# Splitting the double step of a block inverse in two, with a new order table for the merged stage

## The reference

```python
def wkv_scan(r, decay, k, v, a, b, s0):
    def step(s, inp):
        r_t, w_t, k_t, v_t, a_t, b_t = inp
        sa = jnp.einsum('bhvk,bhk->bhv', s, a_t)
        s = s * w_t[:, :, None, :] + sa[..., None] * b_t[:, :, None, :] + v_t[..., None] * k_t[:, :, None, :]
        return s, jnp.einsum('bhvk,bhk->bhv', s, r_t)
```

```python
past = cache_kv[l, page_table].reshape(DB, -1, 4, NSA_KV_HEADS, HEAD_DIM)
```

## Time and profile before

| | |
|---|---|
| median of 3 runs | 2172.32 us (2167.52 to 2173.0) |
| the profiled execution | 2170.53 us |
| its span, first to last instruction | 2168.6 us |
| TensorE matmul busy | 1960.5 us (90%) |
| VectorE busy | 1231.5 us (57%) |
| ScalarE busy | 702.4 us (32%) |
| mean granted TensorE clock | 0.946 |

### The profile page before, as it was taken

One profiled execution on the slowest core, in us unless ns is written; L12 is line 12 of the kernel. 1 busy time (PEld: TensorE's weight loads), 2 busy tenths in 40 slices (PEclk: granted clock), 3 DMA queues, 4 the chain that ended last, 5 costly groups with the idle time before them and its releaser, 6 DMA issues.

```text
span 2168.6 us, 53451 instructions
## 1 busy us (share of the span) xinstructions
PE 1960.5 (90%) x22324; PEld 1804.1 (83%) x22324; DVE 1231.5 (57%) x2034; ACT 702.4 (32%) x1294; POOL 49.2 (2%) x137
## 2 busy tenths in 40 slices
PE   5999999988896999999769998999887979999995
PEld 5999888766696999999769987887666879999995
DVE  3254888887736444452333448888886364444423
ACT  3222333433334232342233223433334332222421
POOL 0000000000000101100000000000000000110000
PEclk9999899998998999999879998999998979999998
DMA  4224733232321323223132256332333212323232
GB/s 181 89 84 144 180 109 105 61 99 83 106 94 45 93 89 97 88 88 98 53 133 89 78 176 160 99 99 71 101 88 110 82 49 89 98 88 96 81 101 79
DMA packets 155835, 214.36 MB, mean 99 GB/s; under 512 B 21569, under 2 KB 121410, under 8 KB 153922
## 3 DMA queue, kind: packets, MB, share of 16 engines
q1 hardware_dynamic: 151682, 208.64, 31.5%
q10 hardware_dynamic: 3904, 2.23, 0.5%
HBM read 202.57 MB, written 16.59 MB: 101 GB/s over the span
## 4 chain that ended last, share of the span: by engine, by line
PE 64%; DVE 18%; SPq 8%; issue 4%; ACT 3%; DMA 3%; DVEq 0%; ACTq 0%; another core or an unknown queue 0%
PE ps L814 17%; PE ps L816 16%; PE ps L815 16%; SPq L704 7%; PE ps L1166 2%; DMA ring<-in_w 1%; DVE arena L1999 1%; PE ps L833 1%; DVE arena L1767 1%; DVE arena L1990 1%; PE ps L834 1%; DVE x L2179 1%; DVE arena L1904 1%; PE ps L1132 1%; PE ps L1047 1%
## 5 line engine op out<-in xcount | busy, mean ns | idle before, releaser
L1678 DVE TENSOR_TENSOR ring_lo<-ring,ring_hi 128x1024 fp32r<-128x1024 f32 x202 | 247.4, 1225 | 679.9 <-ACT ring_hi L1321 679.4
L814 PE MATMUL ps<-hm_hi,ring_hi 128*128 128x260 f32 x1600 | 456.1, 285 | 10.0 <-DVE hm_lo L1685 5.2
L816 PE MATMUL ps<-hm_hi,ring_lo 128*128 128x260 f32 x1600 | 454.7, 284 | 0.0
L815 PE MATMUL ps<-hm_lo,ring_hi 128*128 128x260 f32 x1600 | 453.3, 283 | 0.0
L1321 ACT ACTIVATE ring_hi<-ring 128x1024 fp32r<-128x1024 f32 x202 | 213.8, 1059 | 680.2 <-PE ps L816 615.7
L814 PEld LDWEIGHTS ps<-hm_hi,ring_hi 128*128 128x128 f32 x1600 | 304.1, 190 | 12.5 <-issue 7.3
L816 PEld LDWEIGHTS ps<-hm_hi,ring_lo 128*128 128x128 f32 x1600 | 303.7, 190 | 0.0
L815 PEld LDWEIGHTS ps<-hm_lo,ring_hi 128*128 128x128 f32 x1600 | 303.7, 190 | 0.0
L814 PE MATMUL ps<-in_hi,ring_hi 128*128 128x260 f32 x736 | 211.6, 287 | 6.9 <-DVE ring_lo L1678 6.9
L814 PE MATMUL ps<-hf_hi,ring_hi 128*128 128x260 f32 x704 | 202.1, 287 | 8.8 <-DVE hf_lo L1685 8.2
L816 PE MATMUL ps<-in_hi,ring_lo 128*128 128x260 f32 x736 | 207.8, 282 | 0.0
(11 more groups left out here) (401 smaller groups left out, 3354.5 us busy)
## 6 DMA issues: line engine op xcount, KB each, us to landing
ring<-in_w SPq DMA_DIRECT2D x202, 512.0 KB, 3.5
extra<-in_kv_cmp SPq DMA_DIRECT2D x96, 128.0 KB, 2.3
arena<-in_kv_cmp SPq DMA_DIRECT2D x80, 128.0 KB, 2.4
slot<-in_kv_cmp SPq DMA_DIRECT2D x80, 128.0 KB, 2.9
out_win_old<-in_win SPq DMA_DIRECT2D x16, 511.0 KB, 4.4
arena<-in_k_sel SPq DMA_DIRECT2D x96, 64.0 KB, 1.9
extra<-in_k_sel SPq DMA_DIRECT2D x96, 64.0 KB, 1.9
slot<-in_v_sel SPq DMA_DIRECT2D x96, 64.0 KB, 1.9
```

The source lines that it names most:

```text
L814: mmul(out, wh, hi[:, k, cols], start=(k == 0), stop=False)
L815: mmul(out, wh, lo[:, k, cols], start=False, stop=False)
L816: last = mmul(out, wl, hi[:, k, cols], start=False, stop=(ci == len(chunks) - 1 and k == k1 - 1))
L1678: v.tensor_tensor(ring_lo[:, n % RING, :], r, ring_hi[:, n % RING_HI, :], SUB).then_inc(S["w_lo"], 1)
```

## The change

The step `dbl` is split in `dblw` (bank 1, for the transposed inverse `ww`) and `dblz` (bank 0, for the inverse `zz`), and `add` in `addw` and `addz`. Level 5 has only the z half. The next level's `inv` waits for `addw` alone; `dblw` and `dblz` of a level wait for `addz` of the level before. The semaphores are now `inv_dw` and `inv_z` for w, `inv_d` and `inv_zz` for z. The same matmuls and adds are done. The order table is new as a whole.

```diff
         for lv in range(1, LEVELS):
-            put(("inv", lv), "PE", 1.08, *here(("add", lv - 1) if lv > 1 else "w0", ("maskb", 1)))
+            put(("inv", lv), "PE", 1.08, *here(("addw", lv - 1) if lv > 1 else "w0", ("maskb", 1)))
+            if lv > 1:
+                put(("addz", lv - 1), "DVE", 0.8, *here(("dblz", lv - 1)))
             put(("qmask", lv), "DVE", 0.84, *here(("inv", lv)))
-            put(("dbl", lv), "PE", 2.06 if lv < LEVELS - 1 else 1.05, *here(("qmask", lv), "zz", ("maskk", 1)))
-            put(("add", lv), "DVE", 1.43 if lv < LEVELS - 1 else 0.85, *here(("dbl", lv)))
+            if lv < LEVELS - 1:
+                put(("dblw", lv), "PE", 1.05, *here(("qmask", lv), ("maskk", 1), ("addz", lv - 1) if lv > 1 else "zz"))
+                put(("addw", lv), "DVE", 0.8, *here(("dblw", lv)))
+            put(("dblz", lv), "PE", 1.05, *here(("qmask", lv), ("addz", lv - 1) if lv > 1 else "zz", ("maskk", 1)))
+        put(("addz", LEVELS - 1), "DVE", 0.85, *here(("dblz", LEVELS - 1)))
...
-                    elif stage[0] == "dbl":
+                    elif stage[0] in ("dblw", "dblz"):
                         lv = stage[1]
                         if lv == 1:
                             pe.wait_ge(*at_sc("zz_ok", 1))
                             pe.wait_ge(*at_sc("gmask", 4))
+                        else:
+                            pe.wait_ge(*at_sc("inv_zz", lv - 1))
                         pe.wait_ge(*at_sc("inv_qc", lv))
                         for cj in range(2 * RJ):
                             c, j = divmod(cj, RJ)
                             for r in HP:
-                                last = mmul(ps[r, 0, cj * CH:(cj + 1) * CH], qq[r, c, j, :], zz[r, c, j, :], start=True, stop=True)
-                                if lv < LEVELS - 1:
+                                if stage[0] == "dblz":
+                                    last = mmul(ps[r, 0, cj * CH:(cj + 1) * CH], qq[r, c, j, :], zz[r, c, j, :], start=True, stop=True)
+                                else:
                                     last = mmul(ps[r, 1, cj * CH:(cj + 1) * CH], zz[r, c, j, :], qq[r, c, j, :], start=True, stop=True)
-                        last.then_inc(T["inv_d"], 1)
+                        last.then_inc(T["inv_d" if stage[0] == "dblz" else "inv_dw"], 1)
...
-                        pe.wait_ge(*at_sc("inv_z", LEVELS))
+                        pe.wait_ge(*at_sc("inv_zz", LEVELS - 1))
...
-                    elif stage[0] == "add":
-                        lv = stage[1]
-                        dve.wait_ge(*at_sc("inv_d", lv))
+                    elif stage[0] == "addw":
+                        dve.wait_ge(*at_sc("inv_dw", stage[1]))
+                        o.go(v.tensor_tensor(w8, w8, bank8(1), ADD))
+                        o.tell(T["inv_z"])
+                    elif stage[0] == "addz":
+                        dve.wait_ge(*at_sc("inv_d", stage[1]))
                         o.go(v.tensor_tensor(z8, z8, bank8(0), ADD))
-                        if lv < LEVELS - 1:
-                            o.go(v.tensor_tensor(w8, w8, bank8(1), ADD))
-                        o.tell(T["inv_z"])
+                        o.tell(T["inv_zz"])
```

In the table, the first line of digits is this:

```diff
-ORDER = ("008670667870768677066086067707700667767767777666070707668676070667786607700000777701716817177181767106167171718776717171"
+ORDER = ("807600786067708707760707706670777677078066707766708676776660876700670070707061617167161777107117687171161677187676176678"
```

More of the change, by code:

```diff
@@ L143 @@
           "gmm": 4, "gmask": 4, "nmm": 1, "inv_q": LEVELS - 1, "inv_qc": LEVELS - 1,
-          "inv_d": LEVELS - 1, "inv_z": LEVELS, "zz_ok": 1, "tm_mm": 3, "tm_ev": 3, "rh_mm": 2, "rh_ev": 2, "u_mm": 2,
+          "inv_d": LEVELS - 1, "inv_dw": LEVELS - 2, "inv_zz": LEVELS - 1, "inv_z": LEVELS - 1, "zz_ok": 1, "tm_mm": 3, "tm_ev": 3, "rh_mm": 2, "rh_ev": 2, "u_mm": 2,
           "u_ev": 2, "ds_mm": 2, "s_ok": 2, "y_ev": 1, "mean_mm": 1, "yc": 1, "var_mm": 1, "var_v": 2, "var_a": 1, "done": 1}
@@ L203, in rwkv_threads @@
         for lv in range(1, LEVELS):
-            put(("inv", lv), "PE", 1.08, *here(("add", lv - 1) if lv > 1 else "w0", ("maskb", 1)))
+            put(("inv", lv), "PE", 1.08, *here(("addw", lv - 1) if lv > 1 else "w0", ("maskb", 1)))
+            if lv > 1:
+                put(("addz", lv - 1), "DVE", 0.8, *here(("dblz", lv - 1)))
             put(("qmask", lv), "DVE", 0.84, *here(("inv", lv)))
-            put(("dbl", lv), "PE", 2.06 if lv < LEVELS - 1 else 1.05, *here(("qmask", lv), "zz", ("maskk", 1)))
-            put(("add", lv), "DVE", 1.43 if lv < LEVELS - 1 else 0.85, *here(("dbl", lv)))
+            if lv < LEVELS - 1:
[3 more added lines that the diff above has]
+        put(("addz", LEVELS - 1), "DVE", 0.85, *here(("dblz", LEVELS - 1)))
         for c in range(2):
-            put(("rhs", c), "PE", 1.6, *here(("state", 0) if c else ("add", LEVELS - 1), ("tmcopy", 2)))
+            put(("rhs", c), "PE", 1.6, *here(("state", 0) if c else ("addz", LEVELS - 1), ("tmcopy", 2)))
             put(("rhcopy", c), "ACT", 0.5, *here(("rhs", c)))
@@ L353, in early_thread @@
     return [(("early", 0, "whi"), "ACT", 1.15, [("smp", 6, "sel_v")]), (("early", 0, "wlo"), "DVE", 1.4, [("early", 0, "whi")])]
-ORDER = ("008670667870768677066086067707700667767767777666070707668676070667786607700000777701716817177181767106167171718776717171"
-         "761677877676766232732327732663677227326226872222617766372732726776262363772766672772362762672871161621717672716616671267"
-         "268812672767271167161276212272662866622672827216272772726474624227672272627762642223876677227767827743666237272732473362"
-         "766274633772267632762763273176267266772612772667772711167168261626271221728177617162812627227162786222762622342677262272"
-         "276646222886767264624662488426276766223632362266646663276822363621633687262636682231622171662166221126617711762676171767"
-         "211226212226667627272462762728262726722627428626727627272642726238624266628482736372638372762362263272642422622663322222"
-         "632236226264466744676654646877754767")
+ORDER = ("807600786067708707760707706670777677078066707766708676776660876700670070707061617167161777107117687171161677187676176678"
+         "777717726672336267267676362732762763222632226672622282238626723263212276233611667222212726112227227162661712276821176712"
+         "226776221721762217227222264473686728767662422767242776776272647776676762726277627267632633764276722368477662323812326867"
+         "233672731172276616771672726762276721272672278627122766727162126118617762272721276712212722267727666777672666774263646772"
+         "824467782267627482726267423622278223622622386362426363622262672683222132666822362367626212222621111186626121262221276671"
+         "121162272762612682242676228782222622776667246242772276786247726272762762677227782662622622663227624722623263632738223626"
+         "36282622732662262462647626623276362672683446648467676464655767467677")
 def merged_order():
```

## The result

The changed kernel is slower: 2181.53 us (median of 8 runs, 2179.24 to 2187.32) against 2171.04 us before, ratio 1.0051 with a 95% interval of 1.0041 to 1.0061. One execution in all that follows was slow (3114.87 us, of `split_old_pool`); medians and ratios leave it out. The forecast was 2171 us with a range of 2158 to 2184: the time lies in the range, but the direction is that of rival (b), which had put it at 2183. The profiled execution's span grew from 2168.6 to 2180.6 us.

A forecast was written before the change was run, and what follows sets the result against it. It took VectorE's steps, then SP's page loads, to bound each mixed stage. With `win_v` 0 8 us late, the layers gained 1.3 and 0.1 us: −1.4 on 2170.53, 2170.9 on the median's scale, so 2171 us, range 2158 to 2184.

The forecast's parts named there:

- rival (b): SP's ten units start too late for their pauses to cover, plus a new wait at the fifth `sel_k`: 2183 us, chance 0.24.
- I take `win_v` 0 as 8 us late: First window value product on TensorE, delayed by steps newly ahead on VectorE; 8 us, bounds 5 and 13.
- the end of each stage is the start of that fourth value unit plus 62 us: End of each mixed stage: five value units on SP's queue, of fixed length, follow that unit's start.
- the later of two things: Fourth value unit starts once SP is done with the ten units before it and `sel_v` 0 has been read.
- The steps counted ahead of the last VectorE step: VectorE before `win_v` 0: four moved steps, 8.5 and 1.0 us, and eight split adds, 1.9 us, make 11.4 us more.
- The cover of 2.3 us: Between `win_pt`'s end at 418.06 and `win_v` 0 at 420.32, behind other matmuls; taken off the 11.4 us, leaving 9.1.
- The idle time at the inverse that I gave back: TensorE's waits for VectorE at the `inv` and double lines, 9.3 us a layer, should fall to about 6.
- slack: SP's pause before the fourth value unit, 10.4 and 8.1 us beyond the 1.2, covers a later start of its ten units.
- 0.24 us for each of 16 levels: VectorE's two split add steps of 0.84 us replace one of 1.44, adding 3.8 us a layer.
- Some 3 us lower: If the split cost VectorE nothing, the shift would be 1.9 us smaller and the result some 3 us lower.
- Rival (a): The inverse's chain holds the first half; `win_v` 0 is late by only 3 to 4 us: 2161 us, chance 0.28.
- Rival (c): The split acts on nothing and the table's shifts cancel: 2172 us, chance 0.48 together with the forecast.

The follow-up runs named there:

- `split_old_pool`: Split code in the old order, with every second page transfer of the selected units issued from GpSimd's queue in place of SP's; 2155.91 us, ratio 0.9935.
- `before_late24`: The kernel before with only the sample's steps put later in the merged list, by up to 24 places; 2254.02 us, ratio 1.0396.

## Why the prediction was wrong

Two steps failed: the shift, "I take `win_v` 0 as 8 us late", and the path, "the end of each stage is the start of that fourth value unit plus 62 us", that start being "the later of two things". The shift first. `win_v` 0 is 14.2 us late in the first layer and 16.1 in the second (1519.70 less the layer's later start of 4.6, against 1499.01). Three terms of it:

- The steps counted ahead of the last VectorE step came to 11.4 us and I gave back 1. `win_rr` was 12.3 us late. The sample thread already ran late long before: the fifth from last of its compressed units was issued at 296.83 us instead of 283.90, 12.9 us late, and the unit before it at 269.43 instead of 268.17, only 1.3 us late. I had counted VectorE's steps at the end of the path and not looked for where the lateness begins.
- The cover of 2.3 us was none. It was the chain `win_turn`, `win_pt`, `win_v` 0, read as "other matmuls" since I had the wrong step for `win_pt`; and it grew to 4.2 us, since VectorE and TensorE both had other work between its links. The `state` step that I counted as newly in front had stood inside this chain before.
- The idle time at the inverse that I gave back was of the right kind (9.3 to 7.2, forecast 6), and it was spent at once in other waits.

By the forecast's own rule the rest then follows: the fourth value unit started at 542.43 us, 2.7 later than before, where the forecast had 1.3 earlier, the tail was 62.7 us (forecast 62), the ten units 104.3 (105.6) and SP's second pause 1.2. In the second layer the unit was 11.3 us later, 4.6 of it the layer's start, and the tail 62.8. So on this trace the rule gives the unit's start within 1.4 us with 14.2 and 16.1 in place of 8, and rival (b), with 13 us and 1.5 us at the fifth `sel_k` (2.03 measured), comes within 2 us of the time.

The experiments took the ground from that rule, and so from rival (b) too: that its 2183 lies so near is in part luck. The rule had a limit, the "slack" of 10.4 and 8.1 us, on the assumption that `sel_v` 0 has a time of its own. It has none: with SP's chain 9.5 us later it was 5.9 us later, and the kernel lost 12 us where the rule says 0 to 2. And it said that SP ends the stage: with TensorE's page waits gone the changed order is still 20 us slower (1.0001 against 0.9909).

What the runs put in its place is this. The stage's length follows TensorE, busy for 371 of 415 us, and with the page waits gone the new order loses on it in two ways: the waits for the other engines grow by 1.9 and 2.4 us a layer, and the matmuls, the same in number, are busy for 5.7 and 6.9 us more, by my estimate mostly since more of them fall at the lower clock. In the two kernels of the forecast, which have the page waits, the waits grew by 4.2 and 3.4 us and the busy time by 0.2 and 3.9. The forecast has no term for that: it took the busy time as fixed. My sentence that "TensorE has 43 us of idle time a layer" was read as room; taking single pieces of it away gained nothing. Why the new order lowers the clock more, and which of its steps do it, stays open.

The other steps:

- "0.24 us for each of 16 levels" as a cost of the split: VectorE's busy time rises by 1.6 us a stage (332.9 to 334.4), but the split in the old order takes no more time (1.0005). On the total the Trainium skill's page "VectorE: DVE Perf Modes" (section "The DRAIN you can't avoid"), by which a semaphore more costs nothing extra, came nearer than my row.
- "The first pause of SP longer by 8": it is shorter, 6.1 us instead of 7.1, since the unit ahead of it moved too (420.56 against 406.20).
- "`sel_v` 0 at 536.2 to 537.3": 539.21.
- "Some 3 us lower" without a cost of the split: by the forecast's own sum 1.9 us less shift can lower only the second layer, since `sel_v` 0 holds the first, so at most 1.9.
- The start of the fourth value unit at 538.5: it stands 2.3 us behind the start of `sel_v` 0 in the kernel before, so 538.5 goes with the lower end of "536.2 to 537.3", and the gain of 1.3 us was the most it could be.
- "The other stages the same within 1 us": the stretch between the two mixed stages took 665.0 us against 663.7, so 1.3, and the stretch ahead of the first 186.1 against 187.2.
- Rival (a), faster, is out: the split's gain is real (8 to 10 us) but only where the order keeps TensorE waiting at the levels. Rival (c), no effect, was right for the split in the old order alone.

## What to carry to other kernels

Where one engine is busy for 90% of a stage and takes its work in order, a limit read off another queue (here SP's chain and its pauses) is not independent of it: ask whether the far end of the slack is itself a step on the busy engine. Separate a change of code from the new order that comes with it before explaining either: here they were worth −9 and +21 us, and only their sum was to be seen. A single wait taken out of such an order tends to come back at the next step in line, while work taken off a shared queue (20 us for half of SP's issues in the old order, 11 in the new) stays taken off. And compare TensorE's busy time and granted clock before you lay a difference on waits: with the same matmuls, they carried more than half of it here.

## What the runs showed of the hardware

- On GpSimd's queue one page transfer of 64 KB is issued in 0.54 us (69.07 us for 128 in a stage), about as on SP (0.50 to 0.66: 4.00 to 5.30 us for 8). But a unit's eight take 6.7 us there (425.66 to 432.38 in the rows shown), since about 2 us pass before the last one; SP's eight take 4.9. What GpSimd waits for there the trace does not show. The median from issue to landing is 2.2 to 2.4 us, against 1.9 to 2.2 from SP in the same kernel.
- The order of the same work goes with a different granted clock. With 6048 matmuls in each, a first layer's stage was at the lower level for 40.8, 44.8 and 96.1 us in three orders (the old and the new with shared issue, and `before_late24`), and busy for 364.6, 370.3 and 387.3 us. It is not the order alone: the two layers of the kernel before hold 56.1 and 46.6 us of it.
